# Attention values as the stationary operand: two heads in two column halves, probabilities divided before they are transposed

## The chip, the cores and the metric

The kernel runs on one core of a Trainium2 chip. The metric is the device time of one execution in microseconds (us), the median of three executions. The engines are called by the names of the profile: PE (TensorE; its weight loads are a row kind of their own, PEld), DVE (VectorE), ACT (ScalarE), POOL (GpSimd) and SP (SyncE, which issues the weight DMAs).

## The reference, cut to what matters

The model has four layers of a first block and two of a second, over 256 tokens with 1,024 features. Layer i of the first block is a mixer (attention and an output projection `w_o`) followed by a gated feed-forward. Mixers 0 and 3 are `mixer_a` (a sliding window of 128, 16 query heads over 4 key/value heads, and a sink logit for each head), mixer 1 is `mixer_b` (three dilated groups that are merged), mixer 2 is `mixer_c` (at 256 tokens plain causal attention, 16 heads). Of all three kinds, one head does this:

```python
    s = jnp.einsum('bnqhgd,bnkhd->bnhgqk', qb, kb) * (dh ** -0.5)
    ...
    p = jnp.exp(s - m[..., None])
    l = p.sum(-1)
    if sink is not None:
        l = l + jnp.exp(sk - m)
    o = jnp.einsum('bnhgqk,bnkhd->bnqhgd', p, vb) / jnp.transpose(l, (0, 1, 4, 2, 3))[..., None]
```

The change is about the last line for mixers 0, 2 and 3 (the "sink" mixers and the third mixer), 8 pairs of heads each. The head dimension is 64.

## The kernel before, in words

A class `Order` writes out one list of steps for the whole program. Each engine's program walks that list and issues its part of each step, so every engine has one queue in the order of the list, and semaphores join them. PE's steady work is the weight matmuls: 362 weight tiles of 128x2048 stream in by DMA, ACT rounds each (`hi`, L1581, `whi<-raw`), DVE takes the remainder (`lo`, L1931), and PE runs three matmuls where one would do (L1178 to L1180, L1280 to L1282). Attention is a generator (`attention`, L500s) that is advanced between these matmuls: after each step of weight matmuls (six of them) `pump` first may issue a `lo` and a `hi`, and then resumes the generator n times. n is 5 while a sink mixer projects its last queries, 6 while it runs its output projection, 3 and 5 in the third mixer. One body of the generator takes 7 resumptions (`pace=7`).

Body v of `attention` issues, for pairs of heads, in this order: `pv` of pair v-2 (PE: probabilities times values), `score` of pair v (PE: q times k; DVE: mask, scale and row minimum), `heads` of pair v-2 where there are sinks (DVE: reciprocal of the sums l, and one multiplication for each head out of PSUM into `og`), `probs` of pair v-1 (PE: three transposes of 128x128 for each head; ACT copies head 0's out of PSUM into `PT[0]`, DVE head 1's into `PT[1]`), `exp` of pair v (ACT, four activations with their sums). In the third mixer `heads` comes behind `exp`. Scores and the product with the values share a PSUM bank: columns 0 to 383 for scores, 384 to 511 for the product of the pair two before; bank 4 for the first head of a pair and bank 5 for the second. PE's `pv` of a pair waits until the bank's previous use was read out by DVE.

In `pv` the transposed probabilities are stationary (128x128) and the values move (64 columns), three matmuls for each head; a matmul on f32 operands is two records in the trace. The result has tokens on partitions. `opart`, once for two pairs, therefore turns it: four PE transposes of `og`, an ACT copy into `oh`, a DVE subtraction into `ol` (high and low part for the projection). `tail` issues it a body later and marks the block of 256 features as ready; `project` starts the projection's row steps (`row`, six matmuls on one block) when its block is ready, and until then resumes the generator with no matmuls between.

For each half of the queries, `q_bias` and `rope_v` (DVE) follow the projection of q; `q_bias` also frees the PSUM bank. The projection's accumulators use those same banks 0 to 3. Kind "d" of the second block already divides its probabilities before the transposes, in a DVE step `join` (L2420 to L2429).

Of the kernel before, what the change touches and what calls it, by code (L numbers as in the profile page):

```python
# [11 lines left out]
ALU = mybir.AluOpType  # L12
# [152 lines left out]
class Order:  # L165
# [354 lines left out]
    def attention(self, a, n, mask, ready, consume, kidx, dv, sinks=None, tail=None, pace=7, values=None, weigh=None, before=None, layer=None):  # L520
# [4 lines left out]
        for v in range(n + 2):  # L525
# [13 lines left out]
            if v < n:  # L539
# [4 lines left out]
                for i in range(2):  # L544
# [17 lines left out]
            if v >= 2:  # L562
                if sinks is None:
                    consume(v - 2)
                if v % 2 and tail is not None:
                    due.append(((v - 2) // 2, v))
            for t in range(pace):
                if t == 4 and dv == 128 and v < n:
                    self.counts("joined", (a, v))
                    self.step("join", a, v, layer)  # L570
                yield
        for g, _ in due:
            tail(g)

    def out_part(self, key, source):
# [34 lines left out]
    def mixer_a(self, i):  # L610
        j = i // 3
        u0 = self.units
# [25 lines left out]
        for hh in range(2):  # L638
            u = u0 + hh

            def queries(t, u=u, hh=hh):
                if not t:
                    self.flush()
                self.step("q_bias", u, hh, t)
                rotate("q", u, t)
            self.drive(self.tok_out(("q", u), "a_w_qkv", j, 512 * hh, 2 * i, False, None, queries), 5)
            self.pre.append(turn("q", u, 1))
            if hh:
                break
# [7 lines left out]
            self.side.append(self.attention(u0, 8, "ma", lambda u: ("q", u) in turned, consume,  # L657
                                            lambda v, k: 2 * (v // 4) + (2 * (v % 4) + k) // 4, 64, 16 * j, tail))
        self.project("a_w_o", j, i, ready, self.boundary, 6)
# [7 lines left out]
    def mixer_bc(self, i):  # L667
# [3 lines left out]
        for hh in range(2):  # L671
            for g in range(ng):
# [4 lines left out]
                def heads(u=u, hh=hh, g=g, done=done):  # L677
# [3 lines left out]
                    def consume(gr):  # L681
                        if i == 2:
                            self.step("heads", u, gr, hh)
                        else:
                            self.step("merge", u, gr, g)
# [11 lines left out]
                    def tail(gr):  # L697
                        self.out_part((i, 2 * hh + gr), hh if i == 2 else 0)
                        ready[2 * hh + gr] = True
                    yield from self.attention(u, 4, "mc" if i == 2 else f"mb{g}", lambda u: True, consume,  # L700
                                              lambda v, k: v, 64, None, tail if i == 2 or g == 2 else None,
                                              before=u - 1 if g else None,
# [463 lines left out]
def tensor_program(pe, o, B, sem):  # L1166
# [122 lines left out]
    def rows_ready(a, blk, src):  # L1289
        if src == "o":  # L1290
            b, n = use["opart", a // 2, blk]
            p.wait_ge(f"empty{b}", n + 1)
# [75 lines left out]
    def probs(a, v_):  # L1368
        joined = KIND[a] == "d"
        for i in range(1 if joined else 2):  # L1370
            b, n = use["T", a, v_ + 1, i]
            S = B.S[2 * (v_ % 2) + i]
            if joined:
                p.wait_ge("joined", mark["joined", (a, v_)])
            else:
                p.wait_ge("exp", mark["exp", (a, v_, i)])
# [5 lines left out]
    def pv(a, v_, dv, pairs):  # L1382
# [6 lines left out]
        if KIND[a] == "d":  # L1389
            p.wait_ge(*o.copied[a, v_, 0])  # L1390
            pt, c = B.PT[0], 128 * p_
            for t in range(2):
# [6 lines left out]
                if v_ + 2 >= pairs:  # L1399
                    last.then_inc(sem[f"full{b}"], 1)  # L1400
            return
        for i in range(2):
# [3 lines left out]
            c = 64 * (v_ // 2) if KIND[a] == "a" else 128 * p_ + 64 * i  # L1406
            pt, out = B.PT[i], B.bank[b][:, 384:512]
# [6 lines left out]
    def opart(key, source):  # L1414
        i, blk = key
        b, n = use["opart", *key]
        if i < 4:
            if i % 3 == 0:
                a, v_ = (0, 10)[i // 3], 2 * blk + 3
            else:  # L1420
                a, v_ = (4 + 3 * (blk // 2), 8 + blk // 2)[i - 1], 2 * (blk % 2) + 3
# [149 lines left out]
def scalar_program(ac, o, B, sem, ins):  # L1571
# [328 lines left out]
    def mparts(l, j):  # L1900
# [8 lines left out]
            "parts": parts, "qk_in": qk_in, "v_in": v_in, "turn": turn, "exp": exp, "probs": probs, "rise": rise,  # L1909
            "opart": opart, "unturned": unturned, "silu": silu, "hhi": hhi, "tap": tap, "silu2": silu2,  # L1910
            "gelu_v": gelu_v, "gm_squares": gm_squares, "setup": setup, "tap_b": tap_b, "silu_b": silu_b,
# [8 lines left out]
def vector_program(ve, o, B, sem):  # L1920
# [222 lines left out]

    def heads(a, pair, hh):
        u, p = o.pair(a, pair)
        s = p % 2
        v.wait_ge("exp", mark["exp", (a, pair, 1)])
        i = v.mine(ve.reciprocal(B.rl[:, s, 0:4], B.l[u % 4][:, 4 * p:4 * p + 4]))
        values(a, pair, 1)
        v.wait_ge("own_v", i)  # L2150
        for i in range(2):
            c = 128 * p + 64 * i
            src, gone = values(a, pair, i)
            r = B.rl[:, s, 2 * i:2 * i + 2].unsqueeze(2).broadcast_to([128, 2, 64])
            ve.tensor_tensor(B.og[hh][:, :, c:c + 64], src, r, ALU.mult).then_inc(sem[gone], 1)

# [311 lines left out]
    def mparts(l, j):  # L2468
# [6 lines left out]
            "center": center, "affine": affine, "meansq": meansq, "rms": rms, "sinks": sinks, "scale_x": scale_x, "kv_in": kv_in, "rope_v": rope_v, "q_bias": q_bias,  # L2475
            "score": score, "probs": probs, "heads": heads, "merge": merge, "rise": rise, "weights": weights,
            "opart": opart, "gate": gate, "hlo": hlo, "taps": taps, "gate2": gate2, "gm_squares": gm_squares,
# [9 lines left out]
def pool_program(ge, o, B, sem):  # L2487
# [25 lines left out]
    def rope(key, buf, table):  # L2513
# [5 lines left out]
        for t in range(2):  # L2519
# [122 lines left out]
    def branch(l, b_, d):  # L2642
        if b_ != 1:
            return
        for j in range(2):
# [4 lines left out]

    does = {"loG": lo, "scale_gb": scale_gb, "carry": carry, "rope": rope, "fill": fill,
            "weights": weights, "setup": setup, "xs": xs, "xde": xde, "off": off, "decay": decay, "gate_z": gate_z,
# [73 lines left out]
class Buffers:  # L2726
# [88 lines left out]
    def sm(self, name):  # L2815
        a, n = SMALL[name]
        return self.small[:, a:a + n]

    def act(self, x):

# [13 lines left out]
    def heads_of(self, buf):  # L2834
# [4 lines left out]
        "own_v", "own_a", "own_g", "hi", "loV", "loG", "gone", "xhi", "xnv", "xna", "xg", "stat_v",  # L2839
        "stat_a", "eps", "tables", "rope", "sinks", "filled", "scored", "exp", "joined", "ohi", "merge_g", "silu",  # L2840
        "hhi", "hlo", "cva", "cvv", "gate", "xb", "vnorm", "wdh", "wdl", "lamv", "wst", "dtv", "dav", "xsg", "ea",
# [136 lines left out]
```

## Time and profile before

| | |
|---|---|
| device time, three runs | 2352.62, 2353.83, 2354.62 us (median 2353.83) |
| profiled execution: its own time | 2353.8 us |
| profiled execution: span of the profile | 2352.0 us, granted TensorE clock 0.998 |
| PE busy | 2308.6 us (98% of the span) |
| DVE, ACT, POOL busy | 1453.5 (62%), 1305.4 (56%), 330.6 us (14%) |
| `pv` of mixers 0, 2 and 3 on PE | 46.4 to 94.6, 827.8 to 860.2 and 875.7 to 901.7, 1133.2 to 1181.4 us hold them and their attention |

The views give, for a group of instructions, how long they kept the engine busy, the mean of one in ns, and how long the engine had been idle before them; the timeline gives each instruction's start and length from the start of the span, with equal neighbours merged into one row (their number stands behind x). A matmul's length includes its way through the array, so the next one starts before it ends; what a group costs PE is read from start to start.

### The profile page before, as it was taken

The page shows a single profiled execution, that of the slowest core. Times are in us where ns is not written, and L with a number is a line of the kernel's source. Part 1 is how long each engine was busy: PE and PEld are TensorE (multiplying, and loading weights), DVE is VectorE, ACT ScalarE, POOL GpSimd, SP SyncE. Part 2 cuts the span into 40 slices and gives each one's busy share as a digit, 9 for nine tenths or more (in the row PEclk, how much of TensorE's full clock was granted, in tenths as well). Part 3 has the DMA queues.
Part 4 walks back from the last instruction along what each step waited for, and adds up shares of the span by engine and source line. Part 5 has one row for each costly group of instructions (what it writes and reads, how often), then busy time and mean ns, then how long its engine had stood idle before and what let it go on. Part 6 is the DMA issues. An engine that isn't in the chain of part 4 may idle for free.

```text
span 2352.0 us, 36560 instructions
## 1 busy us (share of the span) xinstructions
PE 2308.6 (98%) x15272; PEld 2067.4 (88%) x15272; DVE 1453.5 (62%) x2217; ACT 1305.4 (56%) x1958; POOL 330.6 (14%) x307
## 2 busy tenths in 40 slices
PE   7999999999999999999999999999999999999999
PEld 5799978888899888998789989899899898998998
DVE  6655555546645546546764567575677686765875
ACT  5554465555544556445564467565665675655654
POOL 0100032212100313001010002343000013530000
PEclk9999999999999999999999999999999999999999
DMA  6255443333455534555345544444455453444553
GB/s 266 90 212 183 179 178 138 141 134 126 179 190 187 197 141 157 196 182 203 113 173 186 194 178 148 144 162 162 179 187 189 175 184 126 162 164 160 201 193 126
DMA packets 58180, 398.92 MB, mean 170 GB/s; under 512 B 6816, under 2 KB 7072, under 8 KB 11680
## 3 DMA queue, kind: packets, MB, share of 16 engines
q1 hardware_dynamic: 56864, 393.75, 46.7%
q8 instruction: 121, 1.98, 0.3%
q10 hardware_dynamic: 1152, 2.83, 0.3%
q14 instruction: 43, 0.35, 0.1%
HBM read 395.51 MB, written 1.05 MB: 169 GB/s over the span
## 4 chain that ended last, share of the span: by engine, by line
PE 82%; DVE 9%; ACT 6%; POOL 2%; issue 1%; DMA 0%; SPq 0%; ACTq 0%; DVEq 0%; POOLq 0%
PE b L1280 12%; PE b L1282 12%; PE b L1281 12%; PE b L1178 12%; PE b L1179 12%; PE b L1180 12%; PE b L1183 5%; DVE wlo L1931 4%; PE b L1187 4%; ACT whi L1581 2%; ACT b L1577 1%; DVE xb L2229 1%; PE b L1246 1%; PE b L1247 1%; ACT S L1578 1%
## 5 line engine op out<-in xcount | busy, mean ns | idle before, releaser
L1931 DVE TENSOR_TENSOR wlo<-raw,whi 128x2048 fp32r<-128x2048 f32 x362 | 845.1, 2339 | 446.4 <-ACT whi L1581 446.1
L1581 ACT ACTIVATE whi<-raw 128x2048 fp32r<-128x2048 f32 x362 | 690.5, 1913 | 426.2 <-PE b L1282 221.9
L1280 PE MATMUL b<-xh,whi 128*128 128x256 f32 x2560 | 723.9, 283 | 1.0 <-DVE wlo L1931 0.7
L1282 PE MATMUL b<-xh,wlo 128*128 128x256 f32 x2560 | 712.4, 278 | 0.0
L1281 PE MATMUL b<-xl,whi 128*128 128x256 f32 x2560 | 711.6, 278 | 0.0
L1280 PEld LDWEIGHTS b<-xh,whi 128*128 128x128 f32 x2560 | 480.3, 188 | 5.6 <-DVE wlo L1931 3.3
L1281 PEld LDWEIGHTS b<-xl,whi 128*128 128x128 f32 x2560 | 481.4, 188 | 1.9
L1282 PEld LDWEIGHTS b<-xh,wlo 128*128 128x128 f32 x2560 | 481.1, 188 | 0.0
L1178 PE MATMUL b<-whi,xh 128*128 128x512 f32 x640 | 262.9, 411 | 1.5 <-DVE wlo L1931 1.5
L1178 PE MATMUL b<-whi,oh 128*128 128x512 f32 x656 | 259.0, 395 | 0.6 <-DVE ol L2220 0.6
L1179 PE MATMUL b<-wlo,oh 128*128 128x512 f32 x656 | 256.1, 390 | 0.0
L1180 PE MATMUL b<-whi,ol 128*128 128x512 f32 x656 | 255.5, 390 | 0.0
L1180 PE MATMUL b<-whi,xl 128*128 128x512 f32 x640 | 250.9, 392 | 0.0
L1179 PE MATMUL b<-wlo,xh 128*128 128x512 f32 x640 | 250.6, 392 | 0.0
L1178 PEld LDWEIGHTS b<-whi,xh 128*128 128x128 f32 x640 | 120.4, 188 | 30.2 <-issue 5.2
L1180 PEld LDWEIGHTS b<-whi,ol 128*128 128x128 f32 x656 | 123.2, 188 | 26.3
L1178 PEld LDWEIGHTS b<-whi,oh 128*128 128x128 f32 x656 | 123.2, 188 | 24.1 <-issue 1.0
L1180 PEld LDWEIGHTS b<-whi,xl 128*128 128x128 f32 x640 | 120.1, 188 | 27.3
L1179 PEld LDWEIGHTS b<-wlo,oh 128*128 128x128 f32 x656 | 123.3, 188 | 22.5
L1179 PEld LDWEIGHTS b<-wlo,xh 128*128 128x128 f32 x640 | 120.5, 188 | 24.3 <-issue 1.9
L1577 ACT ACTIVATE S<-b 128x256 f32<-128x256 f32 (+1 forms) x104 | 43.3, 416 | 165.8 <-PE b L1282 125.7
L2509 POOL TENSOR_TENSOR x<-xn,gt 128x1024 f32<-128x1024 f32 x14 | 33.4, 2384 | 633.6 <-DVE xn L2015 633.6
(238 smaller groups left out, 2904.2 us busy)
## 6 DMA issues: line engine op xcount, KB each, us to landing
raw<-in_w SPq DMA_DIRECT2D x362, 1024.0 KB, 4.8
gt<-in_rows SPq DMA_DIRECT2D x8, 512.0 KB, 4.0
bt<-in_rows SPq DMA_DIRECT2D x8, 512.0 KB, 4.9
abq<-in_rows ACTq DMA_DIRECT2D x2, 768.0 KB, 6.3
x<-in_x SPq DMA_DIRECT2D x1, 1024.0 KB, 6.6
bc<-in_rows SPq DMA_DIRECT2D x4, 256.0 KB, 5.0
out<-x SPq DMA_DIRECT2D x4, 256.0 KB, 2.0
msk<-in_masks SPq DMA_DIRECT2D x1, 768.0 KB, 21.3
```

The lines of the kernel that those rows point to most:

```text
L1178: pe.matmul(out, lh, rh, start=start, stop=False, skip_group_check=True)
L1179: pe.matmul(out, lh, rl, start=False, stop=False, skip_group_check=True)
L1180: return pe.matmul(out, ll, rh, start=False, stop=stop, skip_group_check=True)
L1183: return pe.matmul(out, l, r, start=start, stop=stop, skip_group_check=True)
L1187: return pe.transpose(out, i, B.ident[0:n, 0:n])
L1280: pe.matmul(out, wh[:, k, cs], ah[:, kk, :], start=kk == 0 and s == 0, stop=False, skip_group_check=True)
L1281: pe.matmul(out, wh[:, k, cs], al[:, kk, :], start=False, stop=False, skip_group_check=True)
L1282: last = pe.matmul(out, wl[:, k, cs], ah[:, kk, :], start=False, stop=final and k == 3, skip_group_check=True)
L1577: return ac.activation(out, i, f, bias=bias, scale=scale)
L1581: return ac.activation(out, i, ACT.Copy)
L1931: ve.tensor_tensor(B.wlo[r][:, :], B.raw[r][:, :], B.whi[s][:, :], ALU.subtract).then_inc(sem["loV"], 1)
L2509: i = g.mine(ge.tensor_tensor(B.x[:, t, :], B.xn[:, t, :], B.gt[:, :], ALU.mult))
```

## The change

For mixers 0, 2 and 3 (kinds "a" and "c"):

- A new DVE step `share(v)` takes the reciprocal of the sums and multiplies the probabilities in place, four `tensor_scalar` for each pair; PE's `probs` waits for it instead of for `exp`. It is issued at the fifth of the seven resumptions behind body v.
- `pv` makes the values stationary (128 partitions x 64 columns) and moves the transposed probabilities (128 columns). Head 0 writes partitions 0 to 63 and head 1 partitions 64 to 127; tokens 0 to 127 go to bank 4 and tokens 128 to 255 to bank 5. Six matmuls as before, the two heads alternating.
- The result has features on partitions, so `heads`, and of `opart` the transposes, go. In their place `opair`, once for each pair: two DVE copies of 128x128 out of PSUM, an ACT copy (128x256) into `oh` that waits for both, a POOL subtraction (128x256) into `ol`.
- `consume` (now `opair`) of the third mixer is issued before `probs` and `exp`, as in the sink mixers. A block is ready when its second `opair` has been issued, without the delay of `tail`; a row step waits for POOL's subtraction.

```diff
-            if v >= 2 and sinks is not None:
+            if v >= 2 and KIND[a] in "ac":
                 consume(v - 2)
...
-                if sinks is None:
+                if KIND[a] not in "ac":
                     consume(v - 2)
...
+                if t == 4 and KIND[a] in "ac" and v < n:
+                    for i in range(2):
+                        self.counts("shared", (a, v, i))
+                    self.step("share", a, v)
...
             def consume(v):
-                self.step("heads", u0, v, v // 4)
-
-            def tail(g):
-                self.out_part((i, g), g // 2)
-                ready[g] = True
+                self.out_pair(i, v, u0, v)
+                if v % 2:
+                    ready[v // 2] = True
...
+            for t, k, at in ((0, 0, 0), (1, 0, 128), (1, 1, 256)):
+                b = use["S", a, v_ + 2, t][0]
+                for i in range(2):
+                    c = 64 * (v_ // 2) if KIND[a] == "a" else 128 * p_ + 64 * i
+                    last = mm(B.bank[b][64 * i:64 * i + 64, 384:512], v[:, k, c:c + 64], B.PT[i][:, at:at + 128],
+                              k == 0, k == t)
...
+    def opair(i, pair, first, v):
+        for t in range(2):
+            b, n = use["S", first, v + 2, t]
+            a.wait_ge(f"empty{b}", n + 1)
+        copy(B.oh[:, pair, :], B.opair(pair)).then_inc(sem["ohi"], 1)
...
-    def heads(a, pair, hh):
+    def share(a, pair):
         u, p = o.pair(a, pair)
         s = p % 2
         v.wait_ge("exp", mark["exp", (a, pair, 1)])
         i = v.mine(ve.reciprocal(B.rl[:, s, 0:4], B.l[u % 4][:, 4 * p:4 * p + 4]))
-        values(a, pair, 1)
         v.wait_ge("own_v", i)
         for i in range(2):
-            c = 128 * p + 64 * i
-            src, gone = values(a, pair, i)
-            r = B.rl[:, s, 2 * i:2 * i + 2].unsqueeze(2).broadcast_to([128, 2, 64])
-            ve.tensor_tensor(B.og[hh][:, :, c:c + 64], src, r, ALU.mult).then_inc(sem[gone], 1)
+            S = B.S[2 * (pair % 2) + i]
+            for t, cs in enumerate((slice(0, 128), slice(129, 385))):
+                last = ve.tensor_scalar(S[:, cs], S[:, cs], B.rl[:, s, 2 * i + t:2 * i + t + 1], None, ALU.mult)
+            last.then_inc(sem["shared"], 1)
+
+    def opair(i, pair, a, v_):
+        for t in range(2):
+            b, n = use["S", a, v_ + 2, t]
+            v.wait_ge(f"full{b}", n + 1)
+            ve.tensor_copy(B.opair(pair)[:, 128 * t:128 * t + 128],
+                           B.bank[b][:, 384:512]).then_inc(sem[f"empty{b}"], 1)
...
+    def opair(i, pair, a, v):
+        g.wait_ge("ohi", mark["ohi", (i, "pair", pair)])
+        ge.tensor_tensor(B.ol[:, pair, :], B.opair(pair), B.oh[:, pair, :], ALU.subtract).then_inc(sem["olo"], 1)
```

## Rows read from the trace of the kernel before

**Rows 1.** The page's first part: busy time, share of the span, instructions.
```profile
PE 2308.6 (98%) x15272; PEld 2067.4 (88%) x15272; DVE 1453.5 (62%) x2217; ACT 1305.4 (56%) x1958; POOL 330.6 (14%) x307
```

**Rows 2.** The page's chain that ended last, shares of the span.
```profile
PE 82%; DVE 9%; ACT 6%; POOL 2%; issue 1%; DMA 0%; SPq 0%; ACTq 0%; DVEq 0%; POOLq 0%
```

**Rows 3.** Groups by form: count | busy us, mean ns | idle before, by whom.
```profile
L1183 PE MATMUL b<-v,PT 128*128 128x64 f32 x576 | 69.8, 271 | 1.1 <-DVE og L2174 1.1
...
L1581 ACT ACTIVATE oh<-S 128x256 fp32r<-128x256 f32 x132 | 47.9, 410 | 11.0 <-DVE S L2252 10.2 <-DVE S L2215 0.7
...
L2552 POOL TENSOR_TENSOR og<-og,wsm 128x256 f32<-128x256 f32 x16 | 9.8, 613 | 107.9 <-DVE l L2192 54.9 <-DVE wsm L2198 53.0
...
L2163 DVE COPY og<-b 128x128 f32<-128x128 f32 x16 | 3.8, 282 | 6.2 <-PE b L1183 6.2
```

**Rows 4.** PE's timeline in mixer 0: start us, length us, instruction, [idle before].
```profile
50.03 0.55 PE L1187 MATMUL b<-cst,S 128*128 128x128 f32 x3
...
66.07 0.66 PE L1187 MATMUL b<-cst,xn 128*128 128x128 f32 x4 [1.39 <-DVE xn L2096]
66.56 0.60 PE L1187 MATMUL b<-cst,og 128*128 128x128 f32 x4
66.99 1.45 PE L1183 MATMUL b<-v,PT 128*128 128x64 f32 x12
68.37 0.93 PE L1183 MATMUL b<-kT,qT 64*128 64x128 f32 x8
69.24 0.87 PE L1187 MATMUL b<-cst,S 128*128 128x128 f32 x6
...
78.16 1.45 PE L1183 MATMUL b<-v,PT 128*128 128x64 f32 x12
...
82.50 1.52 PE L1183 MATMUL b<-v,PT 128*128 128x64 f32 x12
```

**Rows 5.** PE's timeline from 68.3 to 68.45 us.
```profile
68.37 0.39 PE L1183 MATMUL b<-kT,qT 64*128 64x128 f32 x2
```

**Rows 6.** DVE's timeline in a body with one row step (mixer 0).
```profile
80.49 0.35 DVE L2125 CUSTOM_DVE_ANT_0 S<-b,msk,nsink 128x128 f32<-128x128 f32 x1 [0.82 <-PE b L1183]
...
81.85 0.17 DVE L2148 RECIPROCAL rl<-l 128x4 f32<-128x4 f32 x1
...
82.47 0.55 DVE L2136 COPY PT<-b 128x384 f32<-128x384 f32 x1
82.93 2.28 DVE L1931 TENSOR_TENSOR wlo<-raw,whi 128x2048 fp32r<-128x2048 f32 x1
85.13 0.34 DVE L2125 CUSTOM_DVE_ANT_0 S<-b,msk,nsink 128x128 f32<-128x128 f32 x1
```

**Rows 7.** ACT's timeline: the last record of exp(0), then the same body.
```profile
50.67 0.19 ACT L1578 ACTIVATION_READ_ACCUMULATOR S<-S,m 128x1 f32 x1
...
80.98 0.49 ACT L1581 ACTIVATE PT<-b 128x384 f32<-128x384 f32 x1 [2.03 <-PE b L1187]
81.37 0.39 ACT L1578 ACTIVATE S<-S,m 128x129 f32<-128x129 f32 x1
...
83.03 0.19 ACT L1578 ACTIVATION_READ_ACCUMULATOR S<-S,m 128x1 f32 x1
```

**Rows 8.** DVE's timeline in the second block: the start of a `join`.
```profile
1575.24 0.18 DVE L2420 RECIPROCAL rl<-l 128x4 f32<-128x4 f32 x1 [1.38 <-ACT S L1578]
...
1575.72 0.55 DVE L2426 TENSOR_SCALAR S<-S,rl 128x128 f32<-128x128 f32 x2
```

**Rows 9.** PE's timeline in the second block: `pv` with 128 moving columns.
```profile
1576.62 0.83 PE L1183 MATMUL b<-v,PT 128*128 128x128 f32 x6
1577.38 0.93 PE L1183 MATMUL b<-kT,qT 64*128 64x128 f32 x8
```

**Rows 10.** DVE's timeline in mixer 0: `q_bias`, with the last of `rope_v`.
```profile
58.58 0.69 DVE L2106 TENSOR_TENSOR xn<-b,abq 128x512 f32<-128x512 f32 x1 [1.04 <-PE b L1180]
...
60.03 0.29 DVE L2096 TENSOR_TENSOR xn<-xn,rtmp 128x128 f32<-128x128 f32 x1
```

More of the change, by code:

```diff
@@ L573, in attention, with out_pair @@
             tail(g)
+    def out_pair(self, i, pair, a, v):
+        self.counts("ohi", (i, "pair", pair))
+        self.counts("olo", (i, pair))
+        self.step("opair", i, pair, a, v)
     def out_part(self, key, source):
@@ L651, in consume @@
             def consume(v):
-                self.step("heads", u0, v, v // 4)
-            def tail(g):
-                self.out_part((i, g), g // 2)
-                ready[g] = True
+                self.out_pair(i, v, u0, v)
+                if v % 2:
+                    ready[v // 2] = True
             self.side.append(self.attention(u0, 8, "ma", lambda u: ("q", u) in turned, consume,
-                                            lambda v, k: 2 * (v // 4) + (2 * (v % 4) + k) // 4, 64, 16 * j, tail))
+                                            lambda v, k: 2 * (v // 4) + (2 * (v % 4) + k) // 4, 64, 16 * j))
         self.project("a_w_o", j, i, ready, self.boundary, 6)
@@ L682, in consume @@
                         if i == 2:
-                            self.step("heads", u, gr, hh)
+                            self.out_pair(i, 4 * hh + gr, u, gr)
+                            if gr % 2:
+                                ready[2 * hh + gr // 2] = True
                         else:
@@ L697, in tail @@
                     def tail(gr):
-                        self.out_part((i, 2 * hh + gr), hh if i == 2 else 0)
+                        self.out_part((i, 2 * hh + gr), 0)
                         ready[2 * hh + gr] = True
                     yield from self.attention(u, 4, "mc" if i == 2 else f"mb{g}", lambda u: True, consume,
-                                              lambda v, k: v, 64, None, tail if i == 2 or g == 2 else None,
+                                              lambda v, k: v, 64, None, tail if g == 2 else None,
                                               before=u - 1 if g else None,
@@ L1290, in rows_ready @@
         if src == "o":
-            b, n = use["opart", a // 2, blk]
-            p.wait_ge(f"empty{b}", n + 1)
+            if a // 2 in (0, 2, 3):
+                p.wait_ge("olo", mark["olo", (a // 2, 2 * blk + 1)])
+            else:
+                b, n = use["opart", a // 2, blk]
+                p.wait_ge(f"empty{b}", n + 1)
         elif src[0] == "h":
@@ L1374, in probs @@
                 p.wait_ge("joined", mark["joined", (a, v_)])
+            elif KIND[a] in "ac":
+                p.wait_ge("shared", mark["shared", (a, v_, i)])
             else:
@@ L1401, in pv @@
             return
+        if KIND[a] in "ac":
+            for t in range(2):
+                b, n = use["S", a, v_ + 2, t]
+                p.wait_ge(*o.copied[a, v_, t])
+                p.wait_ge(f"empty{b}", n)
+            for t, k, at in ((0, 0, 0), (1, 0, 128), (1, 1, 256)):
[4 more added lines that the diff above has]
+                              k == 0, k == t)
+                if k == t and v_ + 2 >= pairs:
+                    last.then_inc(sem[f"full{b}"], 1)
+            return
         for i in range(2):
@@ L1417, in opart @@
         if i < 4:
[L1418 to L1421, printed above, removed]
+            a, v_ = 4 + 3 * (blk // 2), 2 * (blk % 2) + 3
             bo, no = use["S", a, v_, 1]
@@ L1909, in scalar_program @@
             "parts": parts, "qk_in": qk_in, "v_in": v_in, "turn": turn, "exp": exp, "probs": probs, "rise": rise,
-            "opart": opart, "unturned": unturned, "silu": silu, "hhi": hhi, "tap": tap, "silu2": silu2,
+            "opair": opair, "opart": opart, "unturned": unturned, "silu": silu, "hhi": hhi, "tap": tap, "silu2": silu2,
             "gelu_v": gelu_v, "gm_squares": gm_squares, "setup": setup, "tap_b": tap_b, "silu_b": silu_b,
@@ L2148, in heads @@
         i = v.mine(ve.reciprocal(B.rl[:, s, 0:4], B.l[u % 4][:, 4 * p:4 * p + 4]))
-        values(a, pair, 1)
         v.wait_ge("own_v", i)
         for i in range(2):
-            c = 128 * p + 64 * i
-            src, gone = values(a, pair, i)
-            r = B.rl[:, s, 2 * i:2 * i + 2].unsqueeze(2).broadcast_to([128, 2, 64])
-            ve.tensor_tensor(B.og[hh][:, :, c:c + 64], src, r, ALU.mult).then_inc(sem[gone], 1)
+            S = B.S[2 * (pair % 2) + i]
[3 more added lines that the diff above has]
+    def opair(i, pair, a, v_):
+        for t in range(2):
+            b, n = use["S", a, v_ + 2, t]
+            v.wait_ge(f"full{b}", n + 1)
+            ve.tensor_copy(B.opair(pair)[:, 128 * t:128 * t + 128],
+                           B.bank[b][:, 384:512]).then_inc(sem[f"empty{b}"], 1)
     def merge(u, p, g):
@@ L2475, in vector_program @@
             "center": center, "affine": affine, "meansq": meansq, "rms": rms, "sinks": sinks, "scale_x": scale_x, "kv_in": kv_in, "rope_v": rope_v, "q_bias": q_bias,
-            "score": score, "probs": probs, "heads": heads, "merge": merge, "rise": rise, "weights": weights,
+            "score": score, "probs": probs, "share": share, "opair": opair, "merge": merge, "rise": rise, "weights": weights,
             "opart": opart, "gate": gate, "hlo": hlo, "taps": taps, "gate2": gate2, "gm_squares": gm_squares,
@@ L2649, in branch @@
             ge.tensor_tensor(out, out, B.sigs[d][:, 2 * j:2 * j + 2, :], ALU.add).then_inc(sem["mgg"], 1)
-    does = {"loG": lo, "scale_gb": scale_gb, "carry": carry, "rope": rope, "fill": fill,
+    does = {"loG": lo, "scale_gb": scale_gb, "carry": carry, "rope": rope, "opair": opair, "fill": fill,
             "weights": weights, "setup": setup, "xs": xs, "xde": xde, "off": off, "decay": decay, "gate_z": gate_z,
@@ L2817, in sm, with opair @@
         return self.small[:, a:a + n]
+    def opair(self, pair):
+        return self.og[pair // 4][:, pair % 4 // 2, 256 * (pair % 2):256 * (pair % 2) + 256]
     def act(self, x):
@@ L2839 @@
         "own_v", "own_a", "own_g", "hi", "loV", "loG", "gone", "xhi", "xnv", "xna", "xg", "stat_v",
-        "stat_a", "eps", "tables", "rope", "sinks", "filled", "scored", "exp", "joined", "ohi", "merge_g", "silu",
+        "stat_a", "eps", "tables", "rope", "sinks", "filled", "scored", "exp", "joined", "shared", "olo", "ohi", "merge_g", "silu",
         "hhi", "hlo", "cva", "cvv", "gate", "xb", "vnorm", "wdh", "wdl", "lamv", "wst", "dtv", "dav", "xsg", "ea",
```

2 lines of the change are left out of this document (1 added, 1 removed).

## The prediction, made before the changed kernel was run

> **What bounds the kernel now.** I read the first part of the page, then the chain, then PE's timeline through the attention of mixer 0, and last DVE's and ACT's timelines beside it. PE is busy for 98% of the span, the others for 62% and less [rows 1]; of the chain 82% is PE [rows 2]. So PE time saved is time saved, if nothing makes PE wait longer. In the thin stretch of mixer 0, where one row step of six matmuls lies between two bodies, a body takes 82.50 - 78.16 = 4.34 us, all of it PE work [rows 4]. There DVE finishes its score at 81.85, and ACT begins exp already at 81.37, while DVE is still on the second head; exp ends at 83.03 + 0.19 = 83.22 and PE needs it only behind its next `score` [rows 6, 7]. The attention has slack because DVE and ACT overlap. The changed order of their queues is therefore what I look at most.
>
> **PE's own work, removed and added.** *`opart`.* Four transposes cost 66.99 - 66.56 = 0.43 us [rows 4]; 12 calls in three mixers: 5.2 us saved.
>
> *`pv`.* Twelve records take 68.37 - 66.99 = 1.38 us, 0.112 each with the change into `score` in it [rows 4]. Afterwards there are twelve records of 128 moving columns and 64 stationary ones. The trace has none such. The upper bound: with 128 columns and a full array six records and that change take 1577.38 - 1576.62 = 0.76 us [rows 9], so twelve one behind the other take some 0.76 + 6 x 0.112 = 1.43 us, nothing gained. The lower bound: both halves at once. The row halves of `score` do that: two records of the two heads start within 68.37 and 68.45 [rows 5], and all eight, half of them with 256 columns, last 0.93 us [rows 4]. [...] Column halves are nearest to row halves; I take 0.86.
>
> *The change of tiling.* `score` has 128 + 128 + 256 + 256 columns in each half, 0.67 us at 0.112 for 128, but takes 69.24 - 68.37 = 0.87 [rows 4]: 0.2 for going into the row halves and out of them. `pv` in column halves has an entry of its own, half of that, 0.1 us a pair or 2.4 in all; its exit falls together with the entry into `score`. [...]
>
> So a pair saves 1.38 - 0.96 = 0.42 us, 24 pairs 10.1 us, and with `opart` PE's work falls by 15.3 us. Bounds: 5.2 - 3.6 = 1.6 us (one half behind the other) and 18.
>
> **What the other engines get.** `share`: reciprocal and its wait 0.21 us, a 128- and a 256-column `tensor_scalar` 0.55 together, 0.47 from start to start [rows 8]: head 0 is ready 0.76 us after the start, head 1 after 1.23, DVE is free after 1.14. `opair`: two copies of 0.28 [rows 3], 0.49 together; ACT 0.41, of which 0.31 shifts what is behind it (starts follow about 0.1 before the end, as 81.37 after 80.98 + 0.49 [rows 7]); POOL about 0.61 [rows 3]. `heads` and the `opart` of DVE and ACT go. As busy time that is small: DVE gains some 15 us on its 1453.5. As order it is not.
>
> **The new loop.** In the list DVE does score(v), opair(v-2), the PT copy, share(v). ACT does opair(v-2), the PT copy, exp(v). ACT's opair waits for DVE's copies, which are behind the *whole* score(v), so exp no longer overlaps the score. And share(v) waits for exp(v) with score(v+1) behind it in DVE's queue. Follow it once round: score 81.85 - 80.49 = 1.36 [rows 6]; copies 0.49; to ACT 0.04; opair 0.31; PT copy 81.37 - 80.98 = 0.39; exp 83.22 - 81.37 = 1.85 [rows 7]; to DVE 0.04; share 1.14. Sum 5.6 us, whatever PE does. In the third mixer the score is some 0.25 shorter: 5.35 (no row shown, an estimate). PE would need 4.34 - 0.42 = 3.9 us in a thin body and 3.9 + 1.4 = 5.3 in one with twelve matmuls. So a thin body stalls PE by 1.7 us, and the others by 0.3. A `lo` queued between share(v) and score(v+1) adds up to 2.2 (82.93 to 85.13 [rows 6]); before, it filled DVE's idle time.
>
> **Mixer 0 walked through** with these lengths, in times of the trace before. (1) share(0) sits before score(1). exp(0) ends at 50.86 [rows 7]; head 0 is shared at 51.65 and head 1 at 52.1, where PE transposed at 50.03 [rows 4]: PE waits 2.0 in place of 0.55 us. score(1) starts at 52.0 in place of 49.9. (2) A `lo` is ahead of share(1): 56.8 for head 0, PE ready at 55.8: 1.2 us. (3) share(2) waits for exp(2) until 61.7, and behind it now stand q_bias and rope (58.58 to 60.32, 1.74 us [rows 10]) and then score(3), which starts at 64.5. PE waits 0.4. (4) The projection's first row step may come early, since block 0 is ready earlier, and would fill the 1.39 us wait for rope [rows 4]. But its accumulators use the bank that the last q_bias frees, and this q_bias is behind share(3): exp(3) ends at 69.0, share at 70.1, q_bias at 70.85. PE arrives at 66.05, waits 1.5 us for POOL's subtraction and 2.6 for the bank; then the two row steps and the turn of q run to 73.8 (before: 66.56, with no row step done). (5) From there thin bodies, all of them, since the row steps start a body or two earlier: pv(3) 78.5, pv(4) 84.2, then a `lo` before score(6): pv(5) 92.0, pv(6) 97.6, pv(7) 102.3. The waits of (5) sum to 10 us. Before, pv(7) was at 91.5, and one row step (1.4) fewer had been issued. Check by sums: waits 2.0 + 1.3 + 0.4 + 4.1 + 10 = 17.8, before about 3.2 (0.55, 1.39 and small ones), so +14.6; PE work 8 x 0.42 + 4 x 0.43 = -5.1; +9.5, against 102.3 - 91.5 - 1.4 - 0.4 (the last `opart`) = +9.0 by the walk. The last opair (0.5 + 0.4 + 0.6) has three row steps over it and costs nothing. I take +8.8 for a sink mixer, mixer 3 being the same: **+17.6**.
>
> **The third mixer.** First half, twelve to eighteen matmuls between bodies: PE's 5.3 and more meet 5.35; the same walk gives waits of 0.6 (share(0) behind a `lo`) and 0.7, against 4 x 0.42 + 2 x 0.43: -1.0. Second half, thin: waits 0.6, 0.5, 2.6 (score(3) behind a `lo`), 0.8; +1.7. Together **+0.7**.
>
> **Sum**: 2353.8 (the profiled execution's time; span 2352.0 and 1.8 around it, the median of the runs is the same 2353.8) + 17.6 + 0.7 = 2372; the walk takes every queue at its latest, so I say **2371**. Below 0.2% (4.7 us) a measurement of this kernel can't tell a difference from none. PE's pauses stay under 5 us, and I charge no clock: the granted clock was 0.998.
>
> **Rivals.** *The saving arrives* (chance 0.09): DVE idles 38% of the span [rows 1] and PE's reserve covers the longer loop; then -15.3, and -1.4 for each sink mixer's filled rope wait: 2336. It is a single condition: score(v+1) must reach DVE before its share(v) matters, that is the loop must be under 3.9 us. It decides faster once all new waits together are under 15 us. Against it: exp and share alone are 3.0 of them. *Half of it* (0.15): DVE and ACT run ahead of my walk, so that the `lo` (2.2), the bank (2.6) and the first share (1.5) cost nothing: 6.3 less a sink mixer, 2371 - 12.6 = 2358, from 2350 to 2362. *The column halves do not run together* (0.10): PE pays up to 0.57 us more a pair, which the waits of the sink mixers hide in half and the third mixer does not: 16 x 0.28 + 8 x 0.57 = 9: 2380. For it: no row shows column halves at all. Against it: rows 5 have two heads' records starting together though the program issues the first head's four ahead of the second's. [...] *As forecast* (0.66): 2371, its own range 2362 to 2380.
>
> **Chances.** Faster 0.09; within 0.2% half of the "half of it" case and a tail of the forecast: 0.12; slower 0.79. The range leaves out the first rival and the end of the third: 2357 to 2382.
>
> **What would show it.** In the profile after, "PE <- DVE S" at the transposes (L1187) in the waits, some 5 to 8 us a sink mixer; exp of a thin body starting after DVE's copies and not during its score; a body of 5.6 us in the stretch from 75 to 100 us; a PE wait before the first row step of a sink mixer. For PE's part: `pv` and what follows it 0.86 us apart in place of 1.38, and no `cst,og` group in the mixers. The forecast is wrong if the thin body stays near 4.3, or if ACT's opair starts before DVE's score ends.

## The result, and the profile after

The changed kernel takes 2376.69 us (median; 2376.08 to 2377.33) where the kernel before, run beside it, takes 2353.86: a ratio of 1.0098, 95% interval 1.008 to 1.0115. It is slower by 22.8 us. The head of the page and its shares of the chain:

```profile
span 2374.3 us, 36606 instructions
PE 2303.5 (97%) x15224; PEld 2048.9 (86%) x15224; DVE 1469.4 (62%) x2301; ACT 1306.3 (55%) x1970; POOL 354.3 (15%) x331
PE 81%; DVE 9%; ACT 7%; issue 1%; POOL 1%; DMA 0%; ACTq 0%; SPq 0%; DVEq 0%; POOLq 0%
```

Beside [rows 1, 2] this looks like the same kernel: one point less of PE. Averages over 2.3 ms don't show 22 us; the stages do. The groups by form that answer to [rows 3]:

```profile
L1193 PE MATMUL b<-PT,v 128*64 128x128 f32 x288 | 21.0, 281 | 11.4 <-ACT PT L1607 11.2
L2185 DVE TENSOR_SCALAR S<-S,rl 128x256 f32<-128x256 f32 x48 | 16.7, 349 | 0.0
L2180 DVE RECIPROCAL rl<-l 128x4 f32<-128x4 f32 x24 | 4.3, 177 | 38.8 <-ACT S L1604 38.8
```

The reciprocal of `share` is the line to look at. DVE stood idle for 38.8 us in front of 24 of them, 1.6 us each, waiting for ACT's exp; everything queued behind them on DVE stood still as well. What PE waited for in mixer 0, 46.7 to 106 us (us in total, times, longest):

```profile
PE b L1197 <- DVE S L2185: 6.3, 7, 1.7
PE b L1193 <- ACT PT L1607: 4.2, 3, 2.9
PE b L1188 <- DVE xn L2138: 2.2, 1, 2.2
PE b L1188 <- issue: 1.5, 1, 1.5
PE b L1193 <- ACT qT L1607: 0.8, 1, 0.8
```

These are 15.0 us in all. Mixer 3 shows the same lines to 0.1 us. PE's timeline of mixer 0, which answers to [rows 4] (start, length, and in brackets the wait ahead of it with its releaser):

```profile
51.95 1.00 PE L1197 MATMUL b<-cst,S 128*128 128x128 f32 x6 [1.74 <-DVE S L2185]
...
67.96 0.47 PE L1188 MATMUL b<-whi,oh 128*128 128x512 f32 x1 [1.45 <-issue]
...
71.09 0.79 PE L1188 MATMUL b<-whi,oh 128*128 128x512 f32 x1 [2.20 <-DVE xn L2138]
71.69 0.63 PE L1189 MATMUL b<-wlo,oh 128*128 128x512 f32 x1
...
74.23 0.39 PE L1189 MATMUL b<-wlo,oh 128*128 128x512 f32 x1
...
80.27 0.88 PE L1193 MATMUL b<-PT,v 128*64 128x128 f32 x12 [0.58 <-ACT PT L1607]
81.07 0.93 PE L1193 MATMUL b<-kT,qT 64*128 64x128 f32 x8
82.82 1.00 PE L1197 MATMUL b<-cst,S 128*128 128x128 f32 x6 [0.81 <-DVE S L2185]
...
85.91 0.88 PE L1193 MATMUL b<-PT,v 128*64 128x128 f32 x12 [0.69 <-ACT PT L1607]
...
93.75 0.88 PE L1193 MATMUL b<-PT,v 128*64 128x128 f32 x12 [2.90 <-ACT PT L1607]
```

`pv` is followed by `score` after 81.07 - 80.27 = 0.80 us, and no group `cst,og` is left in the three mixers (32 of its 80 records remain elsewhere, from 461 us on). But a thin body now takes 85.91 - 80.27 = 5.64 us, and the next 93.75 - 85.91 = 7.84. DVE and ACT in the same bodies show why; DVE first:

```profile
82.00 0.18 DVE L2180 RECIPROCAL rl<-l 128x4 f32<-128x4 f32 x1 [2.21 <-ACT S L1604]
82.21 1.01 DVE L2185 TENSOR_SCALAR S<-S,rl 128x128 f32<-128x128 f32 x4
83.13 0.35 DVE L2157 CUSTOM_DVE_ANT_0 S<-b,msk,nsink 128x128 f32<-128x128 f32 x1
...
87.64 0.18 DVE L2180 RECIPROCAL rl<-l 128x4 f32<-128x4 f32 x1 [2.21 <-ACT S L1604]
...
88.78 2.28 DVE L1963 TENSOR_TENSOR wlo<-raw,whi 128x2048 fp32r<-128x2048 f32 x1
90.98 0.34 DVE L2157 CUSTOM_DVE_ANT_0 S<-b,msk,nsink 128x128 f32<-128x128 f32 x1
```

```profile
85.06 0.42 ACT L1607 ACTIVATE oh<-og 128x256 fp32r<-128x256 f32 x1 [3.10 <-DVE og L2192]
85.38 0.47 ACT L1607 ACTIVATE PT<-b 128x384 f32<-128x384 f32 x1
85.75 0.39 ACT L1604 ACTIVATE S<-S,m 128x129 f32<-128x129 f32 x1
```

The two engines take turns. ACT idles 3.10 us until DVE has scored both heads and copied the output; then its `opair`, the PT copy and exp run, while DVE, once it has copied its own PT, idles 2.21 us until `share` can begin. Before, exp ran during the score [rows 6, 7].

The change shifts the start of the first `score` of each mixer, read on both traces: mixer 0 costs 10.3 us, the third mixer -1.2 in its first half and +3.3 in its second, mixer 3 with all that follows it up to the second block's first `score` 9.6. Read at single weight matmuls instead, mixer 3 itself costs 10.3 as well, and 0.7 us come back between 1370 and 1400 us, where the change touches nothing. (Every kernel below whose mixer 3 has `share` shows those 0.7 to 0.9 us; the cause is open.) The loss lies in the three mixers that the change touches.

### The profile page after: what moved, and what is told of

The parts are those of the page before. It is cut to its first block, busy times and chain, and to the rows that moved or that the text cites. A ratio compares the mean times of both kernels' runs of the same rounds, so it can differ in the third digit from the quotient of the medians.

```text
span 2374.3 us, 36606 instructions
## 1 busy us (share of the span) xinstructions
PE 2303.5 (97%) x15224; PEld 2048.9 (86%) x15224; DVE 1469.4 (62%) x2301; ACT 1306.3 (55%) x1970; POOL 354.3 (15%) x331
## 4 chain that ended last, share of the span: by engine, by line
PE 81%; DVE 9%; ACT 7%; issue 1%; POOL 1%; DMA 0%; ACTq 0%; SPq 0%; DVEq 0%; POOLq 0%
PE b L1290 13%; PE b L1292 12%; PE b L1291 12%; PE b L1188 11%; PE b L1189 11%; PE b L1190 11%; PE b L1193 4%; DVE wlo L1963 4%; PE b L1197 3%; ACT S L1604 2%; ACT whi L1607 2%; ACT b L1603 1%; PE b L1256 1%; PE b L1257 1%; DVE S L2185 1%
## 5 line engine op out<-in xcount | busy, mean ns | idle before, releaser
L1189 PEld LDWEIGHTS b<-wlo,oh 128*128 128x128 f32 x656 | 124.7, 190 | 22.8
## 6 DMA issues: line engine op xcount, KB each, us to landing
msk<-in_masks SPq DMA_DIRECT2D x1, 768.0 KB, 21.4
```

The lines of the kernel that those rows point to most:

```text
L1189: pe.matmul(out, lh, rl, start=False, stop=False, skip_group_check=True)
```

## The experiments

Two queue orders are under suspicion, and both are in the program's list of steps, so each can be undone by itself. Further kernels take single parts. "Late" below means that ACT's and POOL's `opair` goes behind exp; "next" that `share(v)` stands at the head of body v+1, behind the readiness check and ahead of that body's `score`.

**ACT's step late.** The rest is as changed:

```
 def out_pair: ... self.step("opair", i, pair, a, v)
+        self.outs.append((i, pair, a, v))
 ... behind self.step("exp", ...):
+            while self.outs:
+                self.step("olate", *self.outs.pop(0))
 ACT's and POOL's tables: "opair": opair  ->  "olate": opair
```

> The changed kernel, but ACT's and POOL's part of opair is issued behind exp of the same body; DVE's copies stay where they are. Theory of the loop (ACT's opair holds exp back until the whole score is done): exp then starts 0.9 us after the score again and a round of the loop is 0.88 + 1.85 + 0.04 + 1.14 = 3.9 us in place of 5.6, about what PE needs in a thin body; thin bodies of the sink mixers lose most of their waits (6 to 8 us a sink mixer, 2 in the third), and the half-clock stretches after them go too: 2352 to 2359 us. Rival (share's wait for exp in DVE's queue costs the time by itself): less than 5 us comes back, 2372 or more.

Measured 2355.81 us against 2354.38 beside it, ratio 1.0007 (0.9998 to 1.0016): 21.4 of the 22.8 us are gone. ACT and PE of this kernel in the thin stretch:

```profile
78.26 0.49 ACT L1611 ACTIVATE PT<-b 128x384 f32<-128x384 f32 x1 [1.75 <-PE b L1201]
78.65 0.40 ACT L1608 ACTIVATE S<-S,m 128x129 f32<-128x129 f32 x1
...
80.41 0.40 ACT L1611 ACTIVATE oh<-og 128x256 fp32r<-128x256 f32 x1
```

```profile
76.01 0.88 PE L1197 MATMUL b<-PT,v 128*64 128x128 f32 x12 [0.36 <-DVE PT L2172]
...
80.40 0.88 PE L1197 MATMUL b<-PT,v 128*64 128x128 f32 x12 [0.47 <-DVE PT L2172]
...
86.90 1.55 PE L1197 MATMUL b<-PT,v 128*64 128x128 f32 x12 [2.57 <-DVE PT L2172]
```

exp starts during DVE's score again (which begins at 77.85), and the thin body is back at 80.40 - 76.01 = 4.39 us. The time is in the expected range, but one part of the expectation failed. The changed kernel has five stretches of 3.4 us in its mixers in which TensorE's granted clock is 0.50 (more on them below), and they were expected to go. Here too there are five (52.4, 86.5, 895.5, 1141.3 and 1175.4 us), the second as follows (window, its length, busy time and instructions of PE, PEld, DVE, ACT and POOL, granted clock):

```profile
86.50:89.90 3.40, 3.00 (x20) 2.12 (x20) 1.80 (x6) 0.81 (x4) 0.93 (x2) 0.50 0.02 5
```

In this execution mixer 0 is 2.7 us slower than before, the third mixer 1.4 faster and mixer 3 2.8 slower. PE waits longest in mixer 0 for share(0), 1.73 us, and behind a `lo` ahead of a score, 2.57 us before the `pv` of 86.90. Behind each of the two the clock is at half: `pv`, `score` and the transposes from 86.90 to 90.60 take 3.70 us where they took 0.81 + 0.86 + 0.63 = 2.30 from 76.01 on, and the stretch at 52.4 costs about as much. The two prices, some 2.8 us, are as large as the mixer's loss; what PE waits more than before is about what its matmuls save.

**No `share`.** The probabilities are not divided, and `probs` waits for exp alone; the rest is as changed:

```
-                    self.step("share", a, v)
+                    pass
 probs:
-            elif KIND[a] in "ac":
-                p.wait_ge("shared", mark["shared", (a, v_, i)])
```

> The changed kernel without share: the probabilities are not divided by their sums, and probs waits for exp as before. Theory of the loop: DVE's queue no longer waits for exp, so score(v+1) starts when PE is done, and PE is the bound nearly everywhere: 2353.8 less the 15 to 17 us of PE work, plus 2 to 5 for ACT's late exp: 2338 to 2345. Rival (the column halves or the POOL subtraction cost the time): it stays over 2360.

Measured 2340.98, ratio to before 0.9943 (0.9929 to 0.9956): 13.4 us faster than before and some 36 faster than the changed kernel, as the theory of the loop had it. PE's waits in mixer 0 (46.7 to 100 us) are these:

```profile
PE b L1191 <- ACT PT L1603: 2.8, 5, 0.6
PE b L1191 <- ACT qT L1603: 0.8, 1, 0.8
PE b L1195 <- ACT S L1600: 0.7, 2, 0.3
```

4.3 us instead of 15.0, although ACT's `opair` is still ahead of exp. So the matmuls' saving is real, and ACT waiting for DVE costs little while DVE does not wait for ACT. `share` is dear even with ACT's step late: 2355.81 - 2340.98 = 14.8 us, about the whole saving. The further 21.4 us of the changed kernel need both, ACT waiting for DVE and DVE waiting for ACT. This kernel leaves out the wait for exp and DVE's 1.1 us of work a pair together, so how the 14.8 divide between them is open.

**Only the matmuls.** The kernel before, with `pv` alone in column halves; the steps behind it read the old layout, so what they compute is of no use, but they do the same work:

```
+        if KIND[a] in "ac":
+            ...
+            for t, k, at in ((0, 0, 0), (1, 0, 128), (1, 1, 256)):
+                ...
+                for i in range(2):
+                    ...
+                    last = mm(B.bank[b][64 * i:64 * i + 64, 384:512], v[:, k, c:c + 64], B.PT[i][:, at:at + 128], ...)
```

> The kernel before, with only the product with the values changed: values stationary, two heads in the two column halves, written into the same columns; all that follows is as before, so the output is not the reference's (heads and opart work on data of another layout). Theory: PE saves 1.38 - 0.81 - 0.1 = 0.47 us a pair, 24 pairs: 2353.8 - 11 = 2343 (2340 to 2347). Rival (the change of tiling costs as much as it saves, or the saving lands in waits for DVE and ACT): 2350 to 2355.

Measured 2346.83, ratio 0.9968 (0.9956 to 0.998). 7.5 us come, not the 11 expected, though the time is just inside the expected range. `pv` to `score` is 0.80 us, so 24 pairs save 24 x (1.38 - 0.80 - 0.09 for the entry) = 12 us; but in mixer 0 (46.7 to 100 us) PE now waits 1.0 us more for what comes behind, 0.7 for DVE's `ol` and 0.6 for DVE's PT copy among it:

```profile
PE b L1187 <- DVE ol L2218: 0.7, 1, 0.7
PE b L1183 <- DVE PT L2150: 0.6, 1, 0.6
```

**The order of `pv`.** The changed kernel issues its twelve matmuls alternating between the heads; here head 0's six come ahead of head 1's:

```
-            for t, k, at in ((0, 0, 0), (1, 0, 128), (1, 1, 256)):
-                for i in range(2):
+            for i in range(2):
+                for t, k, at in ((0, 0, 0), (1, 0, 128), (1, 1, 256)):
 ...
```

> The changed kernel, with the six matmuls of pv issued head by head (three of head 0, then three of head 1) in place of in turns. If the two column halves run as streams of their own, as the row halves of score do, the group still takes 0.81 us to the next one and the time stays within 2 us of 2376.7. If PE keeps the order of the program, only one pair of neighbours can overlap: about 1.4 us a group, and 2380 to 2390.

One run: 2382.08, 27.7 above the median of before and 5.4 above the changed kernel's. PE at a `pv` with no wait ahead of it:

```profile
60.88 1.15 PE L1193 MATMUL b<-PT,v 128*64 128x128 f32 x12
61.95 0.93 PE L1193 MATMUL b<-kT,qT 64*128 64x128 f32 x8
```

1.07 us, between the 0.80 of the alternating order and the 12 x 0.112 = 1.34 of one behind the other. The time fits the second theory, the group neither. The single records say why (which head one belongs to is read off their spacing): head 0's six start at 60.88, 61.04, 61.15, 61.26, 61.36 and 61.47, head 1's at 61.15, 61.31, 61.42, 61.53, 61.64 and 61.75. Each half runs at its own pace of about 0.11, and head 1's stream starts 0.27 us behind head 0's in place of together with it; 0.80 + 0.27 is the 1.07. Over 24 pairs that is 6.5 us, against 5.4 measured in one run.

**`share` in the next body, with and without ACT late.** To the first experiment's kernel ("both"), and to the changed kernel ("next only"):

```
             while v == 2 and values and not values():
                 yield
+            if 1 <= v <= n and KIND[a] in "ac":
+                ...
+                self.step("share", a, v - 1)
 ...
-                if t == 4 and KIND[a] in "ac" and v < n:
-                    ...
-                    self.step("share", a, v)
```

> ACT's and POOL's part of opair behind exp, and share(v) no longer issued at the fifth resumption but at the head of body v+1, behind the check that the next queries are turned, so behind every lo, q_bias and rope that was issued meanwhile. Theory: a lo now runs while DVE would wait for exp, and the last q_bias no longer stands behind share(3). The 2.6 us wait of pv(5), the half-clock stretch after it and the 1.4 us wait in the first row step of a sink mixer go: 2 x 4 to 6 us less than with the first edit alone (2355.8): 2344 to 2350. Rival (the place of share does not matter, the round of the loop does): 2353 to 2356.

> The changed kernel with share(v) at the head of body v+1, ACT's opair left ahead of exp. The loop of 5.6 us stays, but the lo ahead of score(6) (2.2 us and a half-clock stretch) and the bank wait of the first row step (2.2 us and a half-clock stretch) go from both sink mixers, the lo ahead of score(3) from the third: 2376.7 less 10 to 14: 2363 to 2367. If only the order on ACT counts: 2374 or more.

Both: 2351.19 against 2353.81, ratio 0.9988 (0.9979 to 0.9997), faster than the kernel before, if barely clear of none. It lies between the range of the theory (up to 2350) and that of its rival (from 2353), so neither holds as it was put. Of the five half-clock stretches in the mixers four are gone; the one behind share(0) of mixer 0 stays, at 52.2. Next only: 2361.05, ratio 1.0031 (1.0018 to 1.0043), 2 us better than expected. PE's waits in mixer 0, of "both" (46 to 98 us), and then of "next only" (46 to 104 us):

```profile
PE b L1201 <- DVE S L2189: 4.4, 4, 1.7
PE b L1197 <- DVE PT L2172: 1.7, 4, 0.5
...
```

```profile
PE b L1197 <- DVE S L2185: 7.8, 7, 1.7
PE b L1193 <- ACT PT L1607: 2.7, 4, 0.7
...
```

In both kernels, the 2.2 us for the bank (`DVE xn`) are gone, since q_bias and `lo` no longer stand behind a waiting `share`. "Next only" keeps the loop, which is why 9.9 us of difference lie between them. Each measured from the kernel before beside it, ACT late brings the loss of 22.8 us to 1.4, next alone to 7.2, and both to a gain of 2.6: 21.4, 15.6 and 25.4 us of gain over the changed kernel. The two overlap, as two edits to one loop do.

**The first `share`.** Its 1.7 us of wait are the largest left. "Both", with share(0) behind score(1):

```
-            if 1 <= v <= n and KIND[a] in "ac":
+            if 2 <= v <= n and KIND[a] in "ac":
 ... behind score(v):
+            if v == 1 and KIND[a] in "ac":
+                ...
+                self.step("share", a, v - 1)
```

> Both edits, and share(0) issued behind score(1) in body 1, so that DVE does score(1) while ACT does exp(0). PE still waits for share(0) as long; exp(1) and with it share(1) come 1 to 2 us earlier, which PE needs only if it waits for share(1): 0 to 2 us less than with the two edits. If PE's wait for share(0) grows because DVE does the score first: up to 1 us more a mixer.

Measured 2355.67, ratio 1.0007 (0.9998 to 1.0016): 4.5 us slower than "both", outside what was expected. PE in the third mixer:

```profile
835.25 1.00 PE L1205 MATMUL b<-cst,S 128*128 128x128 f32 x6 [1.96 <-DVE S L2193]
...
837.03 0.63 PE L1196 MATMUL b<-whi,xh 128*128 128x512 f32 x1
837.46 0.63 PE L1197 MATMUL b<-wlo,xh 128*128 128x512 f32 x1
```

share(0) is now late by a score, so PE waits 1.96 us where "both" waited 0.35, and behind that the weight matmuls come 0.43 apart in place of 0.23: the granted clock is 0.50 from 836.5 to 839.9 (1.00 before and behind it). The wait's price was thus more than its length. The whole loss lies in the third mixer (4.8 us in the two profiled executions, 3.2 of them in its first half); the two sink mixers are 0.5 and 0.3 us faster than in "both".

Two kernels then keep PE busy over it: three more portions of filler ahead of probs(0), once with share(0) behind score(1) and once ahead of it:

```
+                for _ in range(3):
+                    yield
```

> Both edits, share(0) behind score(1), and three resumptions more between score(1) and probs(0), so that PE has a weight step while exp(0) and share(0) run. The wait of 1.7 us before the first transposes of a sink mixer falls to about 1, and no half-clock stretch follows: 2351.2 less 2 to 4: 2347 to 2349. Rival (the weight step taken here is missed later in a thin body): 2351 to 2353.

> As the one before, but share(0) stays ahead of score(1). Shared probabilities are there 0.8 us earlier and score(1) on DVE 2 us later: the first wait falls to about 0.5 us, and body 2 has time to take the later score: 2346 to 2349. Rival: the later score(1) moves the wait to body 2, 2350 to 2353.

Measured 2351.8 (0.9989, 0.998 to 0.9998) and 2353.36 (0.9997, 0.9988 to 1.0006). Mixer 0 gains 1.0 us over "both" in the first of them and no stretch at half clock is left in a mixer, but the third mixer's second half loses 1.8: its filler is spent early and missing later. In both the expected gain did not come; the first falls into the rival's range, the second 0.4 us above it: as far as these two kernels show, filler only moves a wait.

**Readiness.** "Both", with each block marked ready one body later, as in the kernel before:

```
-                if v % 2:
-                    ready[v // 2] = True
+            def tail(g):
+                ready[g] = True
```

> Both edits, but a block is marked ready a body later, as in the kernel before, so that the row steps start later and the last bodies have them. No early row step then fills the wait for rope (1.4 us a sink mixer); instead body 4 comes sooner and one body more has two row steps. If the early row steps are worth their 1.4 us: 2 to 4 us more than with the two edits; if thin bodies are what still costs: 1 to 3 us less.

Measured 2353.43, ratio 0.9999 (0.999 to 1.0008), 2.2 us slower than "both". The loss is in the sink mixers (0.9 and 1.0 us). In mixer 0 the wait for rope of [rows 4] is back, and the waits for `share` are 5.8 us in six in place of 4.4 in four:

```profile
PE b L1201 <- DVE xn L2132: 1.4, 1, 1.4
```

**The third mixer alone.** "Both" in the third mixer; the sink mixers stay as in the kernel before:

```
-            if 1 <= v <= n and KIND[a] in "ac":
+            if 1 <= v <= n and KIND[a] == "c":
 ... and likewise in probs, pv and the order of heads and opart
```

> The sink mixers as in the kernel before; the third mixer changed, with ACT's opair behind exp and share at the head of the next body. In the trace of the kernel with both edits in all three mixers the third mixer gained 2.7 us and the sink mixers 0.8: 2353.8 - 2.7 = 2351, the same within 1 as the kernel with both edits everywhere (2351.2). Rival (the sink mixers' part is worth more than their positions in the trace show): 2353 or more.

Measured 2351.54 against 2354.28, ratio 0.9988 (0.9979 to 0.9996): the third mixer gives 2.7 us by itself, as much as "both" gives in all three. In the sink mixers even the mended order pays for `share` what the matmuls save.

## Why the prediction was right

It said 2371 and slower, by a loop between DVE and ACT; 2376.7 was measured. Its steps one by one:

- *PE's own work.* `pv` was taken at 0.86 us and takes 0.80 to 0.81. No run shows the 0.1 us by which the 0.86 exceeds the 0.76 of [rows 9]: in the changed kernel the second record of a half starts 0.16 us behind the first where the further ones are 0.11 apart (80.27, 80.43, 80.54). The entry into column halves was taken at 0.1, and the last filler matmul ahead of it is spaced 0.32 in place of 0.23 (60.50 to 60.82), so 0.09. The third rival, halves that do not run together, is refuted by the twelve records: they take 0.80 us, where one behind the other, at 0.112 each, would be 1.34.
- *The loop.* 5.6 us summed, 5.64 measured; with a `lo` between share and score, 7.8 walked, 7.84 measured. The rows of ACT and DVE show its links, and the first experiment shows the cause: taking ACT's `opair` out of it brings the body to 4.39.
- *The walk of mixer 0.* It put pv(3), pv(4), pv(5), pv(6) and pv(7) at 78.5, 84.2, 92.0, 97.6 and 102.3. They start at 80.27, 85.91, 93.75, 99.41 and 104.29. All are 1.7 to 2.0 late, and constantly so: the error was made before pv(3), the steps between are right to 0.2 us. share(0) costs 1.74 (2.0 said), share(1) 0.93 (1.2 said), share(2) 0.19 (0.4), the wait ahead of the first row step 1.45 (1.5), the bank behind share(3) 2.20 (2.6). All waits together are 15.0 us, not 17.8; from pv(3) on they are 7.6 and not 10, and yet this part takes 24.0 us where the walk had 23.8, because PE's own work took longer there: transposes that wait between the two heads take 0.76 us in place of 0.63, and one body ran at half clock.
- *The mixers.* +10.3, +2.1 and +10.3 measured, +8.8, +0.7 and +8.8 forecast. The 0.7 us that come back behind mixer 3 no term of the forecast had.

**The mis-sized term** is "PE's pauses stay under 5 us, and I charge no clock". The 5 us was the author's own bound, which no run shows: the longest pause in the three mixers is 2.90 us, and the granted clock falls to 0.50 all the same. Two such stretches of mixer 0 (window, its length, then busy time and instructions of PE, PEld, DVE, ACT and POOL, then the granted clock):

```profile
71.00:74.20 3.20, 3.10 (x7) 2.48 (x8) 3.10 (x6) 0.00 (x0) 0.00 (x0) 0.50 0.00 0
94.70:98.10 3.40, 3.24 (x16) 2.42 (x17) 2.58 (x14) 0.76 (x4) 0.00 (x0) 0.50 0.00 0
```

The changed kernel has five in its mixers (70.8, 94.7, 907.1, 1169.9 and 1193.8 us, 3.4 us each), the kernel before none there. Their price is read off the matmuls. From 71.09 to 74.23 seven weight matmuls take 3.14 us, where at full clock the first behind a wait takes 0.31 (67.96 to 68.27) and the others 0.23, 1.69 in all: 1.4 us lost. Mixer 3 shows the same at 1170.3; in the third mixer five weight matmuls and slower transposes give 1.5. The two at 94.7 and 1193.8 cost nothing: pv(5) to pv(6) is 99.41 - 93.75 = 5.66, the loop's length, so the slow matmuls fill time that PE would have waited. Together 4.3 us; the three mixers grew by 22.7 where the forecast summed 18.3. (The spans grew by 2374.3 - 2352.0 = 22.3: 0.3 more ahead of mixer 0, 0.7 less behind mixer 3.) That the sums meet is arithmetic over two traces; no run held the clock up with the waits in place, so the clock's share is worked out and not shown by itself. The first experiment points the same way: with five stretches left, mixer 0 loses about what two of them cost. The experiment with share(0) behind the score is the nearest to a test of a single one: a wait longer by 1.6 us cost the first half of the third mixer 3.2.

Two smaller points. POOL's subtraction was taken at 0.61 us and takes 0.73 in most places (five of the 24, each beside a `lo` of DVE's, take 2.2 to 2.9 and lift the mean to 1.09):

```profile
L2576 POOL TENSOR_TENSOR ol<-og,oh x24: 722/732/2886, 59.8 to 1205.3; 128x256 fp32r<-128x256 f32 x24
67.14 0.72 POOL L2576 TENSOR_TENSOR ol<-og,oh 128x256 fp32r<-128x256 f32 x1 [6.42 <-ACT oh L1607]
```

(The first line has the shortest, the median and the longest in ns.) No thin body waits for it. The one wait put down to it, ahead of the first row step, is 1.45 us, as said; its row names no engine ("issue"), but the subtraction ends at 67.86 and PE starts at 67.96. And "half of it", the 0.15 rival, supposed that the first share, the bank and the `lo` cost nothing; they cost 1.74, 2.20 and 7.84 - 5.64 = 2.20 us of waits, nearly the full price.

What is left open: "both" has 3.9 us of waits more than the kernel before in mixer 0, 1.4 of them at the first transposes (1.74 against 0.33), and no order that was tried removes them without a loss elsewhere. Whether dividing at another place, or on another engine, would free the 13.4 us that the kernel without `share` shows was not tried.

## What to carry to other kernels

When an edit adds a step that waits, write down for every in-order queue what is ahead of it and behind it, and follow the waits round once: two engines that each wait for the other once per iteration set the loop by their sum, here 5.64 us a body, however idle the profile says they are (DVE busy 62% of the span, ACT 55%). A step whose result is wanted late belongs behind the work that others are waiting for; moving one step of ACT behind exp gave back 21 us. And where the bounding engine is at the edge of waiting, count a saving on it only up to the nearest other engine's loop: here 15 us of matmul time became 2.6.

## What the runs showed of the hardware

- The granted clock of TensorE fell to 0.50 for 3.4 us (70.8 to 74.2 of the changed kernel is one such stretch) behind waits of under 3 us, in a kernel where PE is busy for 97% of the span; matmuls of 512 columns then start 0.43 us apart instead of 0.23. In the changed kernel a single wait of 2.90 us did it (93.75), and so did two short ones with little work between them (1.45 and 2.20; 2.65 and 1.67). A single wait of 1.74 (51.95) did not there; in the kernel with ACT's step late one of 1.73, at the same place, did.
- Column halves of the array ran together: the twelve records of `pv` (128 columns, f32) take 0.80 us alternating, and 1.07 head by head, where the second half's stream starts 0.27 us late.
- DVE's four `tensor_scalar` on `S` take 1.01 us in the changed kernel and 1.48 where POOL's subtraction starts before the second of them, as here in the kernel with ACT's step late:

```profile
80.75 1.48 DVE L2189 TENSOR_SCALAR S<-S,rl 128x128 f32<-128x128 f32 x4
```

```profile
80.89 0.73 POOL L2580 TENSOR_TENSOR ol<-og,oh 128x256 fp32r<-128x256 f32 x1 [3.37 <-ACT oh L1611]
```

  POOL's own time is 0.73 either way. In that kernel the `tensor_scalar` on 256 columns takes 0.82 us in all 15 places where it starts beside a running subtraction that no `lo` delays, and it ends 0.15 us behind the subtraction; elsewhere it takes 0.35. Beside a `lo` of DVE's it is POOL that waits: its subtraction then takes up to 2.9 us and ends 0.6 us behind the `lo`, which keeps its 2.28. These two rows are from the changed kernel:

```profile
105.42 2.28 DVE L1963 TENSOR_TENSOR wlo<-raw,whi 128x2048 fp32r<-128x2048 f32 x1
106.09 2.21 POOL L2576 TENSOR_TENSOR ol<-og,oh 128x256 fp32r<-128x256 f32 x1 [2.01 <-ACT oh L1607]
```

  So of these two pairs the one that starts later is held up, the `tensor_scalar` by 0.47 us of the 0.67 left of the subtraction, the subtraction by 1.48 us of the 1.61 left of the `lo`, and the first is not. The 0.47 us that `share` loses to this are about what separates the thin body of 4.39 us from the 3.9 expected for its loop; no run tested that.
